# Streamed weight blocks laid out contiguously by the host: a cast load of 128 runs of 4 KB in place of 1024 runs of 512 B

## The chip, the cores and the metric

The kernel runs on all 8 cores of one Trainium2 chip, the same program on each. A core takes one prompt sequence of 2048 tokens and 16 of the 128 sampled sequences (8 tokens each, 128 rows), so 2176 rows in all; the weights are read whole by every core, each from its own copy in device memory. No data passes between cores. The metric is the device time of one execution in microseconds, that of the slowest core.

## What is computed

One layer of a convolutional decoder, cut to what matters here:

```python
u = _rmsnorm(h, g_mix)
proj = jnp.einsum('ntd,de->nte', u, w_in)       # 1024 -> 9 * 1024 columns
a_b, a_c, a_h, a_z, b_v, b_g, b_z, gate_a, gate_b = jnp.split(proj, SPLITS, axis=-1)
ya = a_b * _causal_dwconv(ext_a, w_conv_a) * silu(a_z)        # 3 taps over a_c * a_h
ya = einsum(ya, w_out_a)
c = _causal_dwconv(ext_b, w_conv_b) + b_conv_b                # 31 taps over b_v * sigmoid(b_g)
yb = silu(_layernorm(c, ln_g, ln_b)) * silu(b_z)
yb = einsum(yb, w_out_b)
h = h + einsum(sigmoid(gate_a) * ya + sigmoid(gate_b) * yb, w_o)
h = h + sigmoid(_rmsnorm(h, g_ple) @ w_pg) * (p @ w_pe)       # then a last RMSNorm
```

All inputs and outputs are float32 in device memory; the matmuls run in bfloat16, with channels on the partitions.

## The kernel before

**Blocks and stages.** The 2176 rows are taken in three blocks: 768, 768 and 640 rows (512 of the prompt and the 128 sampled ones), each in two column pieces (512 + 256, in the last block 512 + 128). A block goes through stages: s1 loads rows of `x`, takes their RMS and transposes them into `uT`; s2 makes the value and gate of branch B for a chunk of 128 channels (matmuls on L508) and applies the 31 taps as 32 small matmuls (L571), two jobs later than the projection of the same job; s3 makes the four projections of branch A (L687) and s4, two chunks after each s3 chunk from the fifth on, the gate `b_z` with the LayerNorm (L643); s5 makes both output projections and both merge gates (L779, L784, L790); s6 does `w_o`, the second RMSNorm, `w_pg`, `w_pe` (L844, L891, L897) and the store, 128 rows at a time.

**The weights that are streamed.** `w_in`, `w_out_a` and `w_out_b` don't stay on the core. They come as blocks of 1024 rows by 128 columns, cast from float32 to bfloat16 by the DMA, into a ring of 8 tiles `ring0` to `ring7` (128 partitions x 8 x 128 bfloat16). Each of the three blocks streams 88 of them: 8 groups of 2 in s2, 8 groups of 4 in s3, 8 groups of 1 in s4 and 8 groups of 4 in s5, 264 loads in the whole program. `add_group` writes the list of sources in the order of use; `wgroup` hands out the ring tiles of the next group; `wdone` marks a group as used when its last matmul is emitted and calls `pump`, which emits up to four more loads whose ring tiles are free.

**The queues.** The loads are issued by GpSimd (POOL, L288), in program order with the small copies and statistics that POOL does. A rule with four names (`swq`) makes each POOL load wait for the fourth POOL load ahead of it. SyncE (SP) issues the plain loads and stores: `x` rows (L400, L766, L824), the history `sb` and `sa`, the results, and in s2 four SBUF-to-SBUF copies per job that lay the shifted rows out for the 31 taps (`R` from `vext`, L542). `w_o`, `w_pg` and `w_pe` are loaded once, by POOL, during the first chunks of s2 in the first block (`w_o` and `w_pg` in halves of 512 rows with 4 KB of contiguous source each).

**The source of one streamed block before.** `wcol` gives a slice of 128 columns of the row-major matrix, which is 1024 pieces of 512 B that lie 36 KB apart (4 KB apart in `w_out_a` and `w_out_b`).

Of the kernel before, what the change touches and what calls it, by code (L numbers as in the profile page):

```python
# [11 lines left out]
D = 1024  # L12
NCH = 8
# [131 lines left out]
def build_program():  # L145
    nc = bass.Bass("TRN2", target_bir_lowering=False)

    def din(name, shape):
        return nc.dram_tensor(name, shape, F32, kind="ExternalInput").ap()
# [5 lines left out]
    p_d = din("p", [NTOK, 256])  # L155
    sa_d = din("sa", [32, D])
    sb_d = din("sb", [480, D])
    w_in = din("w_in", [D, 9 * D])
    w_oa = din("w_oa", [D, D])
    w_ob = din("w_ob", [D, D])  # L160
    w_o = din("w_o", [D, D])
    w_pg = din("w_pg", [D, D])
    w_pe = din("w_pe", [256, D])
# [11 lines left out]
    with contextlib.ExitStack() as st:  # L175
# [18 lines left out]
        ring = [sb(f"ring{i}", [128, NCH, 128], BF16) for i in range(NRING)]  # L194
# [65 lines left out]
        def add_group(srcs):  # L260
            WG.append(list(range(len(WL), len(WL) + len(srcs))))
            for sap in srcs:
                WL.append((sap, len(WG) - 1))

        def wcol(c0, j):
            return w_in[:, c0 * D + 128 * j:c0 * D + 128 * j + 128]

        for _bi in range(len(BLOCKS)):
            for j in range(NCH):
                add_group([wcol(4, j), wcol(5, j)])  # L270
            for j in range(NCH):
                add_group([wcol(1, j), wcol(2, j), wcol(0, j), wcol(3, j)])
                if j >= 4:
                    add_group([wcol(6, 2 * (j - 4))])
                    add_group([wcol(6, 2 * (j - 4) + 1)])
            for j in range(NCH):
                add_group([w_oa[:, 128 * j:128 * j + 128], w_ob[:, 128 * j:128 * j + 128], wcol(7, j), wcol(8, j)])
        wst = dict(nl=0, ng=0, done=set())

        def pump(maxn=4):  # L280
            nem = 0
            while nem < maxn and wst["nl"] < len(WL) and (wst["nl"] < NRING or WL[wst["nl"] - NRING][1] in wst["done"]):
                nem += 1
                t = wst["nl"]
                wst["nl"] += 1
                k = t % NRING
                src = WL[t][0]
                S.add("pool", lambda e, k=k, src=src: e.dma_start(  # L288
                    out=ring[k][:, :, :], in_=src.rearrange("(k p) m -> p k m", p=128)),
                    writes=[f"ring{k}", swq()], dma=f"ring{k}")  # L290

        def wgroup():
# [44 lines left out]
        for h in range(2):  # L337
            RESIDENT.append(lambda h=h: S.add("pool", lambda e: e.dma_start(
                out=wo_t[:, 4 * h:4 * h + 4, :],
# [687 lines left out]
```

How the kernel before makes its waits and increments, by code:

```python
            def run(engname, e):  # L101
                waited = {}
                for o in ops:
                    if o["eng"] != engname:
                        continue
                    need = {}
                    for d in o["deps"]:
                        od = ops[d]
                        v = od["seq"] * (16 if od["dma"] is not None else 1)
                        if v > need.get(od["chan"], 0):
                            need[od["chan"]] = v
                    for c, v in need.items():
                        if waited.get(c, 0) >= v:
                            continue
                        e.wait_ge(sems[c], v)
                        waited[c] = v
                    ins = o["fn"](e)
                    if o["signal"]:
                        ins.then_inc(sems[o["chan"]], 16 if o["dma"] is not None else 1)
                if engname == final_wait_eng:
                    for c, v in final.items():
                        if waited.get(c, 0) < v:
                            e.wait_ge(sems[c], v)
```

## Time and profile before

| | before |
|---|---|
| time, median of 3 runs (lowest, highest) | 1221.61 us (1203.57, 1291.15) |
| profiled execution: span of the slowest core (core 7) | 1197.9 us |
| spans of the 8 cores in it | 1191.6 to 1197.9 us |
| mean granted TensorE clock, both dies | 0.94 |
| TensorE (PE) busy | 1006.1 us, 84% |
| VectorE, ScalarE, GpSimd busy | 47%, 30%, 28% |
| DMA packets, and those under 512 B | 303514, 278993 |
| read from device memory | 172.23 MB |

The profiled execution has no time of its own beside its span; the lowest of the three runs is 5.7 us above that span. In the rows further down "a<-b" is a transfer or an instruction that writes a from b, with the numbers of ring tiles and buffers left out; the numbers after "x" count. "busy" is the time in which an engine had an instruction in work. A DMA packet's size is that of its written side: a ring load counts as 256 KB although it reads 512 KB of float32. The DMA share is the time of all packets over 16 engines; since an engine can have more than one packet in work, it can come out above 1.

### The profile page before, as it was taken

How to read it: one execution, taken by the hardware profiler on the slowest of the kernel's cores; microseconds unless marked ns; L12 is line 12 of the kernel's file. 1: busy time of each engine (PE TensorE's matmuls, PEld its weight loads, DVE VectorE, ACT ScalarE, POOL GpSimd, SP SyncE). 2: the span in 40 equal slices, each digit the busy share in tenths (PEclk: the TensorE clock that was granted, in tenths of full speed). 3: DMA queues.
4: the chain of work that ended last, by engine and by line, in shares of the span. 5: the costliest groups of instructions: out<-in, count | busy, mean ns of one | idle time of the engine just before them, and what ended most of it. 6: DMA issues, size and time to landing. Idle time of an engine off the chain costs nothing.

```text
span 1197.9 us, 20798 instructions; the slowest of 8 cores (1191.6 to 1197.9 us)
## 1 busy us (share of the span) xinstructions
PE 1006.1 (84%) x6774; PEld 563.1 (47%) x6774; DVE 565.9 (47%) x927; ACT 357.5 (30%) x661; POOL 335.5 (28%) x512
## 2 busy tenths in 40 slices
PE   1599968987999957999889799995799967789984
PEld 0355645544664424556555455542355533444542
DVE  1335426665333553454666533356465665622354
ACT  3122222233112452223222311245222223221243
POOL 4122203323332221122333233313243432323110
PEclk9999989999999977999999899998799998899998
DMA  9798689896998243677889799923498898999321
GB/s 176 122 145 110 107 167 95 81 89 60 104 106 108 79 154 49 90 90 121 81 79 95 69 106 100 114 75 126 72 128 120 78 87 84 90 132 117 36 82 75
DMA packets 303514, 119.74 MB, mean 100 GB/s; under 512 B 278993, under 2 KB 293713, under 8 KB 303377
## 3 DMA queue, kind: packets, MB, share of 16 engines
q0 software_dynamic: 279392, 75.06, 65.0%
q1 hardware_dynamic: 24017, 43.36, 11.7%
q8 instruction: 56, 0.92, 0.3%
q14 instruction: 49, 0.40, 0.1%
HBM read 172.23 MB, written 11.14 MB: 153 GB/s over the span
## 4 chain that ended last, share of the span: by engine, by line
PE 61%; DVE 11%; DMA 10%; issue 9%; ACT 6%; SPq 1%; POOL 1%; DVEq 0%; ACTq 0%; POOLq 0%
PE ps L687 13%; PE ps L571 10%; PE ps L790 9%; PE ps L508 9%; PE ps L891 6%; PE ps L779 4%; DMA t_ring<-w_in 4%; PE ps L784 4%; PE ps L844 3%; DMA t_R_1<-t_vext 3%; DMA t_xs<-x 2%; DVE t_tmp L721 2%; DVE t_tmp L653 1%; DVE t_cbuf L663 1%; ACT t_tmp L661 1%
## 5 line engine op out<-in xcount | busy, mean ns | idle before, releaser
L288 POOL DMA_DIRECT2D t_ring<-w_in x216 | 191.0, 890 | 434.3 <-PE ps L508 196.2
L687 PE MATMUL ps<-t_uT,t_ring 128*128 128x512 bf16 (+2 forms) x1536 | 253.1, 327 | 46.5 <-DMA t_ring<-w_in 17.3
L687 PEld LDWEIGHTS ps<-t_uT,t_ring 128*128 128x128 bf16 x1536 | 142.1, 100 | 156.6 <-issue 65.7
L571 PE MATMUL ps<-t_R_0,t_Wp 128*64 128x512 bf16 (+2 forms) x768 | 135.9, 331 | 9.3 <-DMA t_R_0<-t_vext 9.3
L571 PE MATMUL ps<-t_R_1,t_Wp 128*64 128x512 bf16 (+2 forms) x768 | 134.6, 331 | 7.3 <-DMA t_R_1<-t_vext 7.3
L508 PE MATMUL ps<-t_uT,t_ring 128*128 128x512 bf16 (+2 forms) x768 | 129.5, 324 | 0.3 <-DVE t_uT L426 0.3
L790 PE MATMUL ps<-t_uT,t_ring 128*128 128x512 bf16 (+2 forms) x768 | 129.5, 323 | 0.0
L571 PEld LDWEIGHTS ps<-t_R_0,t_Wp 128*64 128x64 bf16 x768 | 77.0, 113 | 53.8 <-issue 21.7
L891 PE MATMUL ps<-t_wpg_t,t_u2T 128*128 128x512 bf16 x272 | 74.3, 436 | 29.8 <-DVE t_u2T L867 20.8
L508 PEld LDWEIGHTS ps<-t_uT,t_ring 128*128 128x128 bf16 x768 | 68.2, 99 | 58.5 <-issue 17.3
L790 PEld LDWEIGHTS ps<-t_uT,t_ring 128*128 128x128 bf16 x768 | 71.0, 99 | 50.9 <-issue 5.2
L801 DVE TENSOR_TENSOR t_tmp<-ps,t_tmp 128x512 f32<-128x512 f32 (+2 forms) x48 | 25.7, 534 | 130.0 <-ACT t_tmp L797 130.0
L571 PEld LDWEIGHTS ps<-t_R_1,t_Wp 128*64 128x64 bf16 x768 | 77.1, 113 | 16.7 <-issue 15.8
L779 PE MATMUL ps<-t_yaT,t_ring 128*128 128x512 bf16 (+2 forms) x384 | 69.8, 326 | 12.8 <-DMA t_ring<-w_in 5.4
L784 PE MATMUL ps<-t_cbuf,t_ring 128*128 128x512 bf16 (+2 forms) x384 | 68.3, 320 | 8.8 <-DVE t_cbuf L663 8.8
L657 ACT ACTIVATE t_tmp<-t_tmp,t_vecs 128x512 f32<-128x512 f32 (+2 forms) x48 | 33.0, 688 | 125.3 <-DVE t_tmp L653 125.3
L797 ACT ACTIVATE t_tmp<-ps 128x512 f32<-128x512 f32 (+2 forms) x48 | 22.7, 473 | 149.9 <-PE ps L790 149.1
L312 POOL TENSOR_SCALAR t_msq<-t_ssq 128x1 f32<-128x1 f32 x51 | 10.7, 210 | 196.8 <-ACT t_xs L309 138.6
L422 PE MATMUL ps<-t_idb,t_xb 128*128 128x128 bf16 x136 | 15.6, 285 | 59.3 <-ACT t_xb L417 59.3
L578 ACT ACTIVATE t_cbuf<-ps,t_vecs 128x512 f32<-128x512 f32 (+2 forms) x48 | 27.0, 563 | 123.5 <-PE ps L571 123.5
L891 PEld LDWEIGHTS ps<-t_wpg_t,t_u2T 128*128 128x128 bf16 x272 | 28.8, 109 | 72.9 <-issue 51.9
L844 PE MATMUL ps<-t_wo_t,t_cbuf 128*128 128x512 bf16 x272 | 61.0, 379 | 0.0
(121 smaller groups left out, 1291.5 us busy)
## 6 DMA issues: line engine op xcount, KB each, us to landing
t_ring<-w_in POOLq DMA_DIRECT2D x216, 256.0 KB, 7.2
t_xs<-x SPq DMA_DIRECT2D x34, 512.0 KB, 4.1
y<-t_yt SPq DMA_DIRECT2D x17, 512.0 KB, 2.7
t_ring<-w_oa POOLq DMA_DIRECT2D x24, 256.0 KB, 6.5
t_ring<-w_ob POOLq DMA_DIRECT2D x24, 256.0 KB, 7.0
t_R_0<-t_vext SPq DMA_DIRECT2D x48, 67.8 KB, 2.0
t_R_1<-t_vext SPq DMA_DIRECT2D x48, 67.8 KB, 2.0
t_wo_t<-w_o POOLq DMA_DIRECT2D x2, 1024.0 KB, 11.0
```

The lines of the kernel that those rows point to most:

```text
L288: S.add("pool", lambda e, k=k, src=src: e.dma_start(out=ring[k][:, :, :], in_=src.rearrange("(k p) m -> p k m", p=128)), writes=[f"ring{k} ...
L508: S.add("pe", lambda e, b=b, kw=kw, k=k, off=off, n=n: e.matmul(ps[:, b, 0:n], lhsT=ring[kw][:, k, :], rhs=uT[:, k, off:off + n], start=(k ...
L571: S.add("pe", lambda e, bc=bc, ds=ds, i=i, g=g, rhs=rhs, n=n: e.matmul(ps[64 * g:64 * g + 64, bc, 0:n], lhsT=Wp[ds][:, 16 * g + i, :], rhs ...
L578: S.add("act", lambda e, bc=bc, j=j, off=off, n=n: e.activation(out=cbuf[:, j, off:off + n], in_=ps[:, bc, 0:n], func=AF.Identity, bias=vc ...
L657: S.add("act", lambda e, tx=tx, tl=tl, j=j, n=n: e.activation(out=tmp[tl][:, 0:n], in_=tmp[tx][:, 0:n], func=AF.Silu, scale=vcol(V_LNG, j) ...
L687: S.add("pe", lambda e, b=b, kw=kw, k=k, off=off, n=n: e.matmul(ps[:, b, 0:n], lhsT=ring[kw][:, k, :], rhs=uT[:, k, off:off + n], start=(k ...
L779: S.add("pe", lambda e, pya=pya, ka=ka, k=k, off=off, n=n: e.matmul(ps[:, pya, 0:n], lhsT=ring[ka][:, k, :], rhs=yaT[:, k, off:off + n], s ...
L784: S.add("pe", lambda e, pyb=pyb, kbb=kbb, k=k, off=off, n=n: e.matmul(ps[:, pyb, 0:n], lhsT=ring[kbb][:, k, :], rhs=cbufb[:, k, 2 * off:2 ...
L790: S.add("pe", lambda e, b=b, kw=kw, k=k, off=off, n=n: e.matmul(ps[:, b, 0:n], lhsT=ring[kw][:, k, :], rhs=uT[:, k, off:off + n], start=(k ...
L801: S.add("dve", lambda e, pya=pya, ta=ta, n=n: e.tensor_tensor(out=tmp[ta][:, 0:n], in0=ps[:, pya, 0:n], in1=tmp[ta][:, 0:n], op=ALU.mult), ...
L844: S.add("pe", lambda e, h=h, k=k, bm=bm, mcol=mcol: e.matmul(ps[:, bm[h], :], lhsT=cbufb[:, k, mcol:mcol + 128], rhs=wo_t[:, k, 512 * h:51 ...
L891: S.add("pe", lambda e, h=h, k=k, bg=bg: e.matmul(ps[:, bg[h], :], lhsT=u2T[:, k, :], rhs=wpg_t[:, k, 512 * h:512 * h + 512], start=(k == ...
```

## The change

The host now hands `w_in`, `w_out_a` and `w_out_b` over as one array of blocks: block n holds the 128 columns n*128 to n*128+127, and in it row p (of 128) holds, one after another, the 8 pieces of 128 values that go to partition p of the ring tile. So a load reads 128 rows of 4 KB that follow on each other (512 KB without a gap) and writes 128 rows of 2 KB. The bytes, the number of loads, the ring, its order, the waits and every instruction on every engine stay as they are: set side by side, the lists of TensorE, VectorE and ScalarE are the same, and that of GpSimd has the same 373 rows in the same order, with `128x1024` in place of `128x8x128` as the shape of the ring loads. `w_o`, `w_pg` and `w_pe` are not touched. The re-layout is done by the host before the launch.

```diff
-    w_in = din("w_in", [D, 9 * D])
-    w_oa = din("w_oa", [D, D])
-    w_ob = din("w_ob", [D, D])
+    w_in = din("w_in", [9 * NCH, 128, D])
+    w_oa = din("w_oa", [NCH, 128, D])
+    w_ob = din("w_ob", [NCH, 128, D])
...
         def wcol(c0, j):
-            return w_in[:, c0 * D + 128 * j:c0 * D + 128 * j + 128]
+            return w_in[c0 * NCH + j, :, :]
...
-                add_group([w_oa[:, 128 * j:128 * j + 128], w_ob[:, 128 * j:128 * j + 128], wcol(7, j), wcol(8, j)])
+                add_group([w_oa[j, :, :], w_ob[j, :, :], wcol(7, j), wcol(8, j)])
...
                 S.add("pool", lambda e, k=k, src=src: e.dma_start(
-                    out=ring[k][:, :, :], in_=src.rearrange("(k p) m -> p k m", p=128)),
+                    out=ring[k][:, :, :].rearrange("p k m -> p (k m)"), in_=src),
                     writes=[f"ring{k}", swq()], dma=f"ring{k}")
...
+    def tiled(w):
+        w = f(w)
+        n = w.shape[1] // 128
+        return np.ascontiguousarray(w.reshape(8, 128, n, 128).transpose(2, 1, 0, 3)).reshape(n, 128, D)
+
+    shared = dict(w_in=tiled(w_in[0]), w_oa=tiled(w_out_a[0]), w_ob=tiled(w_out_b[0]), w_o=f(w_o[0]), w_pg=f(w_pg[0]),
```

## Rows read from the trace of the kernel before

**Rows 1.** The page's part 3, DMA queues: packets, MB written, share of 16 engines
```profile
q0 software_dynamic: 279392, 75.06, 65.0%
```

**Rows 2.** The page's part 4, the chain that ended last, by engine
```profile
PE 61%; DVE 11%; DMA 10%; issue 9%; ACT 6%; SPq 1%; POOL 1%; DVEq 0%; ACTq 0%; POOLq 0%
```

**Rows 3.** Waits of core 7: engine, line, waited for; us in total, times, longest
```profile
PE ps L687 <- DMA t_ring<-w_in: 17.3, 6, 6.6
...
PE ps L571 <- DMA t_R_0<-t_vext: 9.3, 4, 3.7
...
PE ps L571 <- DMA t_R_1<-t_vext: 7.3, 5, 3.1
...
PE ps L779 <- DMA t_ring<-w_in: 5.4, 4, 2.1
```

**Rows 4.** The same view for core 4
```profile
PE ps L571 <- DMA t_R_0<-t_vext: 10.5, 5, 3.7
PE ps L571 <- DMA t_R_1<-t_vext: 10.1, 5, 4.4
...
PE ps L360 <- DMA t_Abuf<-sb: 8.3, 1, 8.3
PE ps L687 <- DMA t_ring<-w_in: 8.0, 3, 5.0
```

**Rows 5.** Core 7's chain in order of time: start us, us, what
```profile
15.61 9.37 DMA t_xs<-x
...
27.36 8.13 DMA t_xs<-x
...
49.00 7.79 DMA t_R_1<-t_vext
...
852.13 5.92 DMA t_R_1<-t_vext
...
979.89 10.14 DMA t_ring<-w_in
...
1062.60 9.24 DMA t_ring<-w_in
```

**Rows 6.** Core 7 by stretch: length, busy us per engine, PEclk, DMA share, GB/s
```profile
301.00:304.00 3.00, 3.00 (x15) 1.37 (x14) 0.69 (x1) 0.60 (x1) 0.00 (x0) 1.00 1.81 179
...
42.00:46.00 4.00, 4.00 (x18) 1.83 (x17) 1.80 (x1) 0.36 (x1) 0.00 (x0) 1.00 1.09 199
981.00:987.00 6.00, 3.08 (x27) 1.75 (x24) 4.40 (x10) 0.90 (x2) 1.74 (x3) 1.00 1.06 88
```

**Rows 7.** The page's part 6, DMA issues: count, KB written, us from issue to landing
```profile
t_ring<-w_in POOLq DMA_DIRECT2D x216, 256.0 KB, 7.2
t_xs<-x SPq DMA_DIRECT2D x34, 512.0 KB, 4.1
...
t_R_0<-t_vext SPq DMA_DIRECT2D x48, 67.8 KB, 2.0
...
t_wo_t<-w_o POOLq DMA_DIRECT2D x2, 1024.0 KB, 11.0
```

**Rows 8.** POOL's groups by shape: count, busy us, mean ns of one
```profile
L288 POOL DMA_DIRECT2D t_ring<-w_in x216 | 191.0, 890 | 434.3 <-PE ps L508 196.2 <-PE ps L687 160.6 <-DMA t_ring<-w_in 30.1
...
L830 POOL DMA_DIRECT2D t_pbt<-p x11 | 6.7, 609 | 0.5
```

**Rows 9.** By stretch as in Rows 6: matmuls after the wait that ended at 990.6
```profile
990.60:996.00 5.40, 5.36 (x13) 1.90 (x14) 2.17 (x5) 1.95 (x4) 1.17 (x3) 0.50 1.12 108
996.00:1002.00 6.00, 6.00 (x52) 3.62 (x51) 1.48 (x3) 1.47 (x3) 0.78 (x2) 0.99 0.00 0
```

**Rows 10.** By stretch: s3 with s4, first block
```profile
206.00:285.00 79.00, 68.43 (x399) 39.43 (x399) 53.02 (x100) 22.35 (x44) 25.07 (x35) 0.98 0.94 88
```

**Rows 11.** DMA issues between 64 and 96 us: count, KB each, median us to landing
```profile
t_R_1<-t_vext SPq DMA_DIRECT2D x6, 35.8 KB, 7.9
```

**Rows 12.** Core 7's chain: two successive chunks of s2 in the second block
```profile
489.40 3.56 PE ps L508 x16
...
500.25 3.56 PE ps L508 x16
```

More of the change, by code:

```diff
@@ L997 @@
     ident = np.eye(128, dtype=np.float32)
-    shared = dict(w_in=f(w_in[0]), w_oa=f(w_out_a[0]), w_ob=f(w_out_b[0]), w_o=f(w_o[0]), w_pg=f(w_pg[0]),
+    def tiled(w):
[3 more added lines that the diff above has]
+    shared = dict(w_in=tiled(w_in[0]), w_oa=tiled(w_out_a[0]), w_ob=tiled(w_out_b[0]), w_o=f(w_o[0]), w_pg=f(w_pg[0]),
                   w_pe=f(w_pe[0]), vecs=vecs, gfin=gfin, ident=ident)
```

## The prediction

> **What bounds the kernel now.** I read the DMA queues first. GpSimd's queue takes 65% of 16 engines' time [rows 1], nearly all of it in ring loads (264 x 1024 = 270336 of its 279392 packets), which looks as if the DMA engines were the bound. The chain that ended last says otherwise: 61% TensorE, 11% VectorE, 10% DMA [rows 2]. So transfers hold the end back for about 120 of 1197.9 us, and only that part can move. Third, the waits of TensorE itself: on core 7 it stood 17.3 + 5.4 = 22.7 us for ring tiles and 9.3 + 7.3 = 16.6 us for the shifted rows `R` [rows 3]; on core 4, whose span is 0.7 us shorter, 8.0 us for ring tiles on L687, 20.6 us for `R` and 8.3 us for `sb` [rows 4]. The reader should see that the cores reach nearly the same end by different waits. Fourth, the chain in order of time shows where the transfers sit: two `x` loads at the start, of 9.37 and 8.13 us; `R` copies of 7.79 us at 49 us and 5.92 us at the start of the third block; ring loads of 10.14 and 9.24 us in the third block [rows 5]. An `x` load takes 4.1 us in the median and an `R` copy 2.0 us [rows 7], so the long ones wait behind something, and in each of those places ring loads are in flight.
>
> Last, the speed of a ring load, by stretch. Between 301 and 304 us ring loads run alone at 179 GB/s written with a DMA share of 1.81. Between 42 and 46 us half of `w_o` runs, with the very rows that the change gives the ring loads (4 KB read, 2 KB written): 199 GB/s at a share of 1.09 [rows 6]. So the share of 65% overstates the occupation: the small packets overlap, and at its best the old form is only 11% slower. But the old form isn't always at its best: between 981 and 987 us, with ring loads waiting and hardly anything else on this core's queues, it moves 88 GB/s [rows 6], half as much. What slows it there is outside this core's queues; that other cores' reads do it is a guess.
>
> **The change part by part.** The order, the waits and the bytes stay. What changes is the packets (264 x 896 = 236544 fewer), the issue and the speed.
>
> Issue: a ring load holds POOL for 890 ns, a `p` load with 128 rows 609 ns [rows 8]. I take 0.6 us, so 264 x 0.29 = 77 us less POOL time. POOL is busy 28% of the span and waits for TensorE most of the rest, so this is worth nothing except ahead of an exposed group of four, 4 x 0.29 = 1.2 us, counted below. If POOL's cover were gone, the whole 77 us would count.
>
> Transfer of one ring load (262144 B written): 1.46 us at 179 GB/s, 3.0 us at 88 GB/s; the new form 1.32 us at 199 GB/s. What the new form does where the old one drops to 88 no row shows. Below: it drops as much, 2.7 us; above: it doesn't drop, 1.32 us. I take 1.5, near the `w_o` row, since that row was read while the other cores loaded their `w_o` too.
>
> By the Trainium skill's page "DMA: Bandwidth & Descriptors", section "Why small descriptors are slow (HBM only)", each packet carries about 3 cycles over size/32; eight packets of 256 B then need 88 cycles and one of 2 KB 67, a factor of 1.31, where the trace has 1.11 between its two undisturbed streams. By the page one load would come to 1.1 us (an estimate), and the sum below would gain at most 2 us more.
>
> A group of four from its first issue to its last landing: now three issues of 0.89 us and the 9.24 us of the last load [rows 5, 8], 11.9 us, while TensorE needs 8.7 us for one s5 group of the third block (32 matmuls of 512 and of 128 columns). New: the first load like an `x` load (the same 128 rows of 4 KB, 4.1 us) plus 0.3 us for the longer issue, then three at 1.4: 8.6 us. Bounds: 8.4 us, and the 11.0 us of `w_o`, which is four such loads in one [rows 7]. I take 8.6, 3.3 us less per exposed group.
>
> Sum for core 7. *Ring waits*: ten, of 22.7 us; the two long ones (6.6 and 4.1 us) shrink by 3.3 each and the other eight, 12.0 us, nearly go: 18 us. After a long wait TensorE runs at a granted clock of 0.50, its lower level, for 5.4 us, then 0.99 [rows 9]; that costs 2.7 us each time. With shorter waits I count 3 us back in all. *Start*: both `x` loads share the engines with the first eight ring loads; alone they would take 4.1 us, so the bounds are 0 and 9.3 us; I take 7, since eight loads at 1.4 us are nearly through when the second `x` load is issued. *R*: the copies stand behind one pair of ring loads (and, four times, behind a piece of `w_o` or `w_pg`, which stays); bounds 0 and 16.6 us; I take half, 8. *sb*: four ring loads ahead of it become shorter; 2 us. Together 38 us.
>
> Core 4 by the same steps: ring 8, clock 1, start 6, `R` 10 of 20.6, `sb` 3 of 8.3: 28 us. The time is that of the slowest core, so the gain is nearer to core 4's: 32 us less the little that cores drift apart. Against span plus surroundings, 1197.9 + 5.7 = 1203.6 us (the lowest run; the median shown is 18 us above it, and I predict for executions like the profiled one), the sum is 1203.6 - 32 = 1171.6, so **1171 us**. Late next is VectorE: in s3 with s4 of the first block TensorE is busy 68.4 of 79 us without a ring wait, the chain running through VectorE and ScalarE [rows 10].
>
> **The rivals.**
>
> *All waits on transfers go.* Ring waits with their clock (22.7 + 5.4), the start (9.3), `R` (16.6) and `sb` (2.4) on core 7 are 56 us; the same on core 4 is about 46. Time 1203.6 - 50 = 1153. For it: 88 GB/s could be the old form's weakness alone. Against it: `w_pg` still stands ahead of `R`, where copies took 7.9 us [rows 11], and after the first projection of a block no work covers the copy.
>
> *The waits pass to VectorE.* If the s3 and s4 ring waits only uncover the chain of rows 10, what remains is s5's 5.4, start 4, `R` 4, `sb` 1: 14 us, time 1189. For it: in the first block the same stage loses 10.6 us of 79 with no ring wait.
>
> *Bytes bound the loads.* The load of a core runs as fast as the memory gives it and the stall at 88 GB/s stays; only the earlier issue counts, 1.2 us for each of six exposed groups: 7 us, time 1196. For it: the undisturbed streams differ by 11%. Against it: 199 GB/s written was reached. The page named above gives, in "Where 436 GB/s comes from", about 358 GB/s per core from HBM as what binds. Ring loads at 179 GB/s written read just 358 GB/s; but `w_o` read 398 GB/s, so the trace bears the rule out only in part.
>
> *Slower: `R` copies starve.* A row of 2 KB holds an engine longer than one of 256 B. In s2 a copy has cover: a chunk takes 500.25 - 489.40 = 10.85 us [rows 12], the copies are issued some 3.2 us into it, so landing within 7.6 us is hidden. Behind `w_pg`, the same rows, they took 7.9 us [rows 11]. If a pair of ring loads did that, and 2 us more, in each of the 24 chunks, 48 us would be lost against 14 won: 1238. It decides from a landing of 7.6 us on. Against it: `w_pg` is as many bytes as four ring loads, a pair half of that, and ahead of `R` there now stand the same bytes in smaller rows.
>
> **How the numbers follow.** Chances: the sum as worked out 0.55 (own range 1160 to 1184), all waits go 0.15, passed to VectorE 0.18, bytes 0.08, starved copies 0.04. The predicted time is that of the first. The range leaves out the lower half of the second case (0.07), most of the fourth (0.06) and the fifth: 1140 to 1197. About 2% is what a measurement of this kernel tells from no change; against 1203.6 that is 1179.5. Four fifths of the first case and the whole second lie below it: 0.60 faster. The third, fourth and the rest of the first make 0.36 the same; slower 0.04.
>
> **What would show it.** Right: GpSimd's queue at 42848 packets and a share near 35% with unchanged MB; ring issues near 0.6 us, landing median near 5 us in place of 7.2; TensorE's waits for ring tiles under 6 us on every core; the two `x` pieces at the start under 6 us; no stretch of ring loads below 150 GB/s. Wrong towards bytes: stretches at 88 GB/s remain. Wrong towards VectorE: ring waits gone, but s3 with s4 of the third block as long as before. Wrong towards starving: `R` landings above 7.6 us outside the first 100 us. The step I trust least is the 1.5 us of a load where the old form drops to 88 GB/s; next is the half that I took for `R`.

## The result, and the profile after

The changed kernel takes 1179.67 us (median of 4 runs, 1177.29 to 1208.40) where the kernel before, on the same chip and in the same series, takes 1219.42 us (median of 4, 1203.57 to 1291.15). The ratio is 0.971 with a 95% interval of 0.964 to 0.978: about 3% faster. On another chip the same kernel came out at 0.978 (experiment e0), so 2 to 3% is what the change is worth. Ratios leave out executions in which the cores of one die run at a lower granted clock, so a median can stand beside a far higher maximum.

| profiled execution | before | after |
|---|---|---|
| span of the slowest core | 1197.9 us (core 7) | 1178.2 us (core 4) |
| span of core 7 | 1197.9 us | 1174.3 us |
| span of core 4 | 1197.2 us | 1178.2 us |
| mean clock of core 7, of core 4 | 0.944, 0.941 | 0.941, 0.949 |
| DMA packets of GpSimd's queue | 279392 | 42848 |

The page of the kernel after, of its slowest core (core 4). The first line is GpSimd's DMA queue (packets, MB written, share of 16 engines), the second the chain that ended last by engine, the last three are DMA issues (count, KB written, median us to landing):

```profile
q0 software_dynamic: 42848, 75.06, 42.1%
...
PE 64%; DVE 11%; issue 9%; ACT 7%; DMA 7%; SPq 1%; DVEq 0%; POOL 0%; ACTq 0%; POOLq 0%
...
t_ring<-w_in POOLq DMA_DIRECT2D x216, 256.0 KB, 5.6
t_xs<-x SPq DMA_DIRECT2D x34, 512.0 KB, 4.2
...
t_wo_t<-w_o POOLq DMA_DIRECT2D x2, 1024.0 KB, 10.3
```

Beside [rows 1, 2, 7]: the packets are those foretold, the bytes are unchanged, a ring load lands in 5.6 us in place of 7.2, and the chain goes through DMA for 7% of the span in place of 10%. An `x` load, whose form didn't change, takes what it took (4.2 us against 4.1), and a half of `w_o` hardly less (10.3 against 11.0).

TensorE's waits for transfers on core 7 (engine, line, waited for; us in total, times, longest), to be read against [rows 3]:

```profile
PE ps L571 <- DMA t_R_1<-t_vext: 8.3, 3, 4.7
PE ps L571 <- DMA t_R_0<-t_vext: 7.3, 3, 3.4
...
PE ps L360 <- DMA t_Abuf<-sb: 3.5, 1, 3.5
...
PE ps L687 <- DMA t_ring<-w_in: 2.0, 1, 2.0
...
PE ps L779 <- DMA t_ring<-w_in: 0.3, 1, 0.3
```

And on core 4, against [rows 4], with one line of the kernel before that [rows 4] doesn't have:

```profile
PE ps L687 <- ACT t_tmp L661: 17.3, 7, 3.5
```

After:

```profile
PE ps L687 <- ACT t_tmp L661: 22.1, 9, 3.0
...
PE ps L571 <- DMA t_R_0<-t_vext: 8.7, 4, 3.6
PE ps L571 <- DMA t_R_1<-t_vext: 7.5, 3, 4.3
...
PE ps L687 <- DMA t_ring<-w_in: 5.2, 4, 1.9
...
PE ps L360 <- DMA t_Abuf<-sb: 4.7, 1, 4.7
```

The waits for ring tiles fell on core 7 from 22.7 to 2.3 us; the waits for `R` hardly moved (16.6 to 15.6 on core 7, 20.6 to 16.2 on core 4). The largest wait of L687 is now, on every core, the one for ScalarE's `t_tmp`: on core 7 it took the place of the ring tiles, on core 4 it was the largest before and grew from 17.3 to 22.1 us.

Where the 19.7 us of span came from. The table is worked out from the two traces: a stage lasts from its first matmul to the first matmul of the next one (a, b, c are the three blocks; s1a counts from the start of the span; s3 is cut at its fifth chunk, where s4 joins in), and each number is the median over the 8 cores.

| us | s1a | s2a | s3a, first half | s2b | s2c | s3c with s4 | s5c | s6c | all others |
|---|---|---|---|---|---|---|---|---|---|
| before | 37.8 | 99.1 | 69.5 | 88.8 | 76.0 | 74.1 | 79.0 | 69.0 | 600.8 |
| after | 35.1 | 95.6 | 67.3 | 87.0 | 74.9 | 70.3 | 74.0 | 70.1 | 599.9 |

The third block's s3 with s4 and its s5, where the ring waits were, gave 8.8 us, the start 2.7, the three s2 stages 6.4, the first half of s3a, where `sb` is waited for, 2.2; s6c, which has no ring load, is 1.1 longer.

What TensorE did with that time, also worked out from the two traces (two cores lack the same 95 matmuls in both, so the busy times are a little low on both sides):

| mean of the 8 cores | before | after |
|---|---|---|
| span, us | 1195.1 | 1173.4 |
| TensorE busy, us | 1006.4 | 998.8 |
| its waits for ring tiles | 13.0 | 3.5 |
| for `R` | 18.9 | 15.3 |
| for `sb` and `sa` | 8.9 | 6.0 |
| for ScalarE (without `xb` of s1) | 34.0 | 38.7 |
| for VectorE | 45.4 | 42.6 |

So 9.5 us came out of the ring waits, and nearly as much, 7.6, out of the matmuls themselves: TensorE needed less time for the same work, since a higher clock was granted to it, on seven of the eight cores. Before:

```profile
die 0 (median of its cores): 1195.3 us, clock 0.941
die 1 (median of its cores): 1194.9 us, clock 0.942
```

and after:

```profile
die 0 (median of its cores): 1173.6 us, clock 0.949
die 1 (median of its cores): 1174.5 us, clock 0.948
```

Half of the 7.6 us lies in s3c with s4. There the ring waits fell from 7.2 to 3.2 us on the mean of the cores and the waits for ScalarE rose from 7.7 to 11.7, so that TensorE stood idle as long as before; what got shorter is its busy time, 59.5 to 55.7 us, at a granted clock of 0.97 in place of 0.91. In s5c the ring waits went from 3.7 to 0.2 and little took their place (the stage is 5.2 us shorter, 0.8 of it busy time).

### The profile page after: what moved, and what is told of

It reads as the page before. It is cut to its first block, busy times and chain, and to the rows that moved or that the text cites. A ratio compares the mean times of both kernels' runs of the same rounds, so it can differ in the third digit from the quotient of the medians.

```text
span 1178.2 us, 20798 instructions; the slowest of 8 cores (1166.8 to 1178.2 us)
## 1 busy us (share of the span) xinstructions
PE 1000.9 (85%) x6774; PEld 562.7 (48%) x6774; DVE 560.9 (48%) x927; ACT 356.5 (30%) x661; POOL 231.0 (20%) x512
## 3 DMA queue, kind: packets, MB, share of 16 engines
q0 software_dynamic: 42848, 75.06, 42.1%
q1 hardware_dynamic: 24017, 43.36, 12.2%
## 4 chain that ended last, share of the span: by engine, by line
PE 64%; DVE 11%; issue 9%; ACT 7%; DMA 7%; SPq 1%; DVEq 0%; POOL 0%; ACTq 0%; POOLq 0%
PE ps L687 13%; PE ps L571 10%; PE ps L790 10%; PE ps L508 9%; PE ps L891 6%; PE ps L779 5%; PE ps L784 5%; PE ps L643 3%; PE ps L844 3%; DMA t_xs<-x 2%; DMA t_R_1<-t_vext 2%; ACT t_tmp L661 2%; DVE t_cbuf L663 2%; DVE t_tmp L653 2%; DVE t_tmp L650 1%
## 5 line engine op out<-in xcount | busy, mean ns | idle before, releaser
L687 PE MATMUL ps<-t_uT,t_ring 128*128 128x512 bf16 (+2 forms) x1536 | 254.6, 328 | 40.8 <-ACT t_tmp L661 22.1
L687 PEld LDWEIGHTS ps<-t_uT,t_ring 128*128 128x128 bf16 x1536 | 143.9, 101 | 150.1 <-issue 53.1
L288 POOL DMA_DIRECT2D t_ring<-w_in x216 | 115.7, 536 | 479.4 <-PE ps L508 213.8
L571 PE MATMUL ps<-t_R_0,t_Wp 128*64 128x512 bf16 (+2 forms) x768 | 132.5, 326 | 8.7 <-DMA t_R_0<-t_vext 8.7
L571 PE MATMUL ps<-t_R_1,t_Wp 128*64 128x512 bf16 (+2 forms) x768 | 131.7, 326 | 7.5 <-DMA t_R_1<-t_vext 7.5
L508 PE MATMUL ps<-t_uT,t_ring 128*128 128x512 bf16 (+2 forms) x768 | 130.3, 325 | 0.3 <-DVE t_uT L426 0.3
L790 PE MATMUL ps<-t_uT,t_ring 128*128 128x512 bf16 (+2 forms) x768 | 128.9, 322 | 0.0
L571 PEld LDWEIGHTS ps<-t_R_0,t_Wp 128*64 128x64 bf16 x768 | 75.8, 111 | 53.2 <-issue 21.1
L571 PEld LDWEIGHTS ps<-t_R_1,t_Wp 128*64 128x64 bf16 x768 | 75.9, 111 | 15.1 <-issue 13.3
L797 ACT ACTIVATE t_tmp<-ps 128x512 f32<-128x512 f32 (+2 forms) x48 | 22.7, 473 | 143.1 <-PE ps L790 142.3
L891 PEld LDWEIGHTS ps<-t_wpg_t,t_u2T 128*128 128x128 bf16 x272 | 28.5, 108 | 74.1 <-issue 52.5
L422 PE MATMUL ps<-t_idb,t_xb 128*128 128x128 bf16 x136 | 15.6, 285 | 56.0 <-ACT t_xb L417 56.0
L643 PE MATMUL ps<-t_uT,t_ring 128*128 128x512 bf16 (+2 forms) x384 | 60.9, 317 | 0.0
## 6 DMA issues: line engine op xcount, KB each, us to landing
t_wo_t<-w_o POOLq DMA_DIRECT2D x2, 1024.0 KB, 10.3
```

Of the source, the lines that this page charges most:

```text
L288: S.add("pool", lambda e, k=k, src=src: e.dma_start(out=ring[k][:, :, :].rearrange("p k m -> p (k m)"), in_=src), writes=[f"ring{k}", swq( ...
L508: S.add("pe", lambda e, b=b, kw=kw, k=k, off=off, n=n: e.matmul(ps[:, b, 0:n], lhsT=ring[kw][:, k, :], rhs=uT[:, k, off:off + n], start=(k ...
L571: S.add("pe", lambda e, bc=bc, ds=ds, i=i, g=g, rhs=rhs, n=n: e.matmul(ps[64 * g:64 * g + 64, bc, 0:n], lhsT=Wp[ds][:, 16 * g + i, :], rhs ...
L643: S.add("pe", lambda e, pz=pz, kz=kz, k=k, off=off, n=n: e.matmul(ps[:, pz, 0:n], lhsT=ring[kz][:, k, :], rhs=uT[:, k, off:off + n], start ...
L687: S.add("pe", lambda e, b=b, kw=kw, k=k, off=off, n=n: e.matmul(ps[:, b, 0:n], lhsT=ring[kw][:, k, :], rhs=uT[:, k, off:off + n], start=(k ...
L790: S.add("pe", lambda e, b=b, kw=kw, k=k, off=off, n=n: e.matmul(ps[:, b, 0:n], lhsT=ring[kw][:, k, :], rhs=uT[:, k, off:off + n], start=(k ...
```

## The experiments

All were compared with the kernel before in runs on the same chip; e0 to e3 share one chip, e4 to e7 a second, e8 to e11 a third. The median of before there was 1210.94, 1211.05 and 1212.47 us, so kernels of different chips are set side by side by their ratio.

### e0: the changed kernel on another chip

> The changed kernel once more, so that the next three have it beside them on one chip. Every theory: 0.971 of the kernel before (0.965 to 0.978), about 1179 us; TensorE's waits for ring tiles 2 to 6 us on each core, its waits for R copies still 12 to 17 us, ring issues 0.53 us each on POOL.

Measured: 1183.29 us, ratio 0.978 (0.973 to 0.983). The two intervals overlap, and the kernels below are set against both ratios, 0.971 and 0.978.

### e1 and e2: packets or distance

The change does two things to a block's source: it makes one packet of eight, and it brings the pieces together. e1 does the second alone, 1024 runs of 512 B that fill 512 KB without a gap:

```diff
-    w_in = din("w_in", [9 * NCH, 128, D])
+    w_in = din("w_in", [9 * NCH, D, 128])
...
-                    out=ring[k][:, :, :].rearrange("p k m -> p (k m)"), in_=src),
+                    out=ring[k][:, :, :], in_=src.rearrange("(k p) m -> p k m", p=128)),
...
```

(`w_oa`, `w_ob` and the host's re-layout follow suit, here and in e2 and e11.)

> The host lays a block out as one piece of 512 KB, but with the packets of the kernel before: 1024 runs of 512 B. Three theories of what made the ring loads slow. Apart (the 512 B pieces lie 36 KB apart in memory): as fast as the changed kernel, ratio 0.97 to 0.98, ring loads never below 150 GB/s for some us. Packets (8 times as many small packets): no gain, 0.99 to 1.0, stretches of 85 to 110 GB/s remain and the landing median stays near 7 us. Issue (0.88 us against 0.53 us of POOL's time for one load): no gain either, 0.99 to 1.0, but with streams near 179 GB/s throughout. In every theory POOL's issue is back at 0.88 us.

e2 does the first alone, 128 runs of 4 KB that lie 288 KB apart:

```diff
-    w_in = din("w_in", [9 * NCH, 128, D])
...
+    w_in = din("w_in", [128, 9 * NCH, D])
...
-            return w_in[c0 * NCH + j, :, :]
+            return w_in[:, c0 * NCH + j, :]
...
```

> The other half: 128 runs of 4 KB, as in the changed kernel, but with the 128 runs of a load 288 KB apart (32 KB in the two output projections). Apart: most of the gain is lost, 0.985 to 1.0. Packets and issue: as the changed kernel, 0.97 to 0.98, issue 0.53 us and landing median 5.6 us.

Measured: e1 1202.05 us, ratio 0.993 (0.990 to 0.996); e2 1184.63 us, ratio 0.979 (0.975 to 0.984). The queue and the landing of a ring load on the page of e1:

```profile
q0 software_dynamic: 279392, 75.06, 64.3%
...
t_ring<-w_in POOLq DMA_DIRECT2D x216, 256.0 KB, 6.3
```

and on that of e2:

```profile
q0 software_dynamic: 42848, 75.06, 42.0%
...
t_ring<-w_in POOLq DMA_DIRECT2D x216, 256.0 KB, 5.4
```

The long runs give the gain wherever they lie; bringing short runs together gives 0.7%. The fewer packets did it, not the neighbourhood.

### e3: is it the cheaper issue?

```diff
+        junk = sb("junk", [128, 240], BF16)
...
+                S.add("pool", lambda e: e.memset(junk[:], 0.0), writes=["junk"])
                 S.add("pool", lambda e, k=k, src=src: e.dma_start(
```

> The changed kernel with a POOL memset of about 0.34 us ahead of each ring load, so that a load costs POOL what it cost before (0.88 us). Issue: the gain goes, 0.99 to 1.0. Apart and packets: at most 4 us slower than the changed kernel, 0.97 to 0.976, since POOL waits for TensorE most of the time.

Measured: ratio 0.980 (0.973 to 0.987). GpSimd's groups (count, busy us, mean ns of one):

```profile
L290 POOL DMA_DIRECT2D t_ring<-w_in x216 | 115.0, 532 | 428.1 <-PE ps L510 203.7 <-PE ps L689 161.1 <-PE ps L645 16.7
L289 POOL MEMSET t_junk<- 128x240 bf16 x264 | 84.2, 319 | 0.0
```

With the fill a load costs POOL 532 + 319 = 851 ns, close to the 890 of before, and the gain is still there. The 0.35 us a load that the change takes off POOL (94 us in all on core 4) are worth nothing that can be measured; the ratio of the changed kernel on this chip is 0.978.

### e11: half way

A block as two halves, 256 runs of 2 KB:

```diff
-    w_in = din("w_in", [9 * NCH, 128, D])
...
+    w_in = din("w_in", [9 * NCH, 256, 512])
...
-                    out=ring[k][:, :, :].rearrange("p k m -> p (k m)"), in_=src),
+                    out=ring[k][:, :, :].rearrange("p (h k) m -> p h (k m)", h=2),
+                    in_=src.rearrange("(h p) m -> p h m", p=128)),
...
```

> Each streamed block lies as two halves of 128 runs of 2 KB (256 runs a load; 1 KB written a run) instead of 128 runs of 4 KB. Theory 'the run costs, whatever its length': the fixed part falls by three quarters where the change takes seven eighths, so nearly all of the gain is there: ratio 0.976 to 0.981, q0 near 42% to 47%, landing near 5.6 us. Rival 'only the longest packets do': a ratio half way to the load of 1024 runs in one place (0.993), 0.984 to 0.988, landing near 6 us.

Measured: 1186.04 us, ratio 0.982 (0.977 to 0.987). Queue, issue and landing on its page:

```profile
q0 software_dynamic: 76640, 75.06, 46.0%
...
L288 POOL DMA_DIRECT2D t_ring<-w_in x216 | 154.1, 716 | 449.3 <-PE ps L509 204.3
...
t_ring<-w_in POOLq DMA_DIRECT2D x216, 256.0 KB, 5.6
```

Share and landing are those of the first theory, the ratio falls between the two ranges. Of the way from e1 (0.993) to the long runs (0.978) it has three quarters, and of the packets it takes away six sevenths; within the intervals that is the same. So it doesn't separate the theories by time.

### e4: what is left in the ring loads

From the ninth load on only an eighth of each block is brought (the matmuls then use stale weights):

```diff
-                S.add("pool", lambda e, k=k, src=src: e.dma_start(
-                    out=ring[k][:, :, :].rearrange("p k m -> p (k m)"), in_=src),
+                nk = NCH if t < NRING else 1
+                S.add("pool", lambda e, k=k, src=src, nk=nk: e.dma_start(
+                    out=ring[k][:, 0:nk, :].rearrange("p k m -> p (k m)"), in_=src[:, 0:128 * nk]),
```

> The changed kernel, but every ring load after the first 8 brings only the first 512 B of each row, an eighth of the bytes (the later matmuls then use old weights, so the results are not the layer's). It asks what all ring transfers together still cost. Theory that transfers still hold the end back (R copies and x rows behind ring loads, the last ring waits): 20 to 28 us less than the changed kernel, ratio to the kernel before about 0.955 to 0.96, waits of TensorE for R under 8 us. Theory that what is left is VectorE's chain and the waits without a ring load in front: at most 8 us less, 0.97 or more.

Measured: 1168.48 us (1166.08 to 1169.57), ratio 0.964 (0.960 to 0.969), between the two expectations. Core 4's waits for transfers, all of them:

```profile
PE ps L572 <- DMA t_R<-t_vext: 6.8, 5, 5.1
PE ps L361 <- DMA t_Abuf<-sb: 3.3, 1, 3.3
PE ps L375 <- DMA t_Abuf<-sa: 1.2, 1, 1.2
```

No ring tile is waited for, on any core, and yet only about 12 us are gained on the changed kernel (1180.63 us on this chip, see e5; by the ratios 8 to 17). By stage the gain is 3.4, 3.9 and 4.0 us in the three s2 and 0.8 in s5c; s3c with s4 takes 70.1 us against 70.3. TensorE's waits for `R` fall from 15.3 to 8.2 us on the mean of the cores. So after the change the ring loads cost their remainder almost wholly by standing ahead of the `R` copies. The third block's s3 with s4 is at its floor: without any ring wait TensorE waits 12.7 us for ScalarE there.

### e5: an experiment that missed

```diff
-                    wdone(wg_)
+                    if j == 0:
+                        wst["done"].add(wg_)
+                    else:
+                        wdone(wg_)
```

> The changed kernel, but the two ring loads that the first chunk of each block sets free are issued with those of the second chunk, so that the first R copies of a block have no ring load in front. Theory that R copies wait behind ring loads whatever their rows: the pieces of some 5.2 us at the start of the second and third block become 2 to 3 us, 2 to 3 us less for each block, 5 to 8 us less in all than the changed kernel. Rival, that the copies are late by themselves (their issue on SP, the first use): no change within 2 us and landings still near 5 us.

Measured: 1180.63 us, ratio 0.974 (0.970 to 0.978), every stage within 0.7 us of the changed kernel. It says nothing on its question: the two loads moved behind other work in the order of emission, but POOL had nothing to do in between, and issued them (core 4) at 455.82 and 456.69 us, beside the first `R` copies as before; the copy on the chain still took 5.18 us at 456.96 us. To hold a load back it needs a wait (e8). So e5 is in effect the changed kernel on the second chip.

### e6: the start

The first eight ring loads go out as four at the start and two after each of the first `x` tiles. Here two go out at the start and the other six from the fourth `x` tile on:

```diff
-        pump()
+        pump(2)
...
-            pump(2)
+            if tl[0][0] > 0 or ti >= 3:
+                pump(2)
```

> The changed kernel, but at the start only two ring loads are issued at once and the other six after the fourth tile of x rows. Theory that the x rows of the start stand behind ring loads: the pieces of 7.5 and 5.7 us in the chain become 4.1 to 4.5 us, and s2 begins 4 to 5 us earlier. Rival, that the other cores' reads of x or the serial work on ScalarE set the pace: at most 1 us.

Measured: 1177.97 us, ratio 0.975 (0.968 to 0.982). The `x` loads issued between 14 and 24 us in e6, core 4 (count, KB, median us to landing):

```profile
t_xs<-x SPq DMA_DIRECT2D x3, 512.0 KB, 3.5
```

and in the kernel after between 14 and 30 us, with the four ring loads that went out beside them:

```profile
t_xs<-x SPq DMA_DIRECT2D x3, 512.0 KB, 7.5
t_ring<-w_in POOLq DMA_DIRECT2D x4, 256.0 KB, 8.8
```

s1a goes from 35.1 to 30.9 us with s2a as before (95.9). Over the 8 cores these three `x` loads took 9.5, 9.1 and 6.7 us in the kernel before, 7.5, 8.1 and 5.5 after, and 3.5 to 3.6 in e6: of what they lost beside ring loads, the longer rows took off less than a third, and the order takes off all. That the whole kernel gains by it is not separated from its interval.

### e7: `w_o` and `w_pg` in pieces

Sixteen loads of 128 rows, one with each job of s2 from the fourth on (two from the fifteenth), in place of four loads of 512 rows in the first chunks:

```diff
-                out=wo_t[:, 4 * h:4 * h + 4, :],
-                in_=w_o[512 * h:512 * h + 512, :].rearrange("(k p) m -> p k m", p=128)),
+                out=wo_t[:, q, :], in_=w_o[128 * q:128 * q + 128, :]),
...
+                if bi == 0 and 3 <= idx:
+                    for _ in range(1 if idx < 14 else 2):
+                        if RESIDENT:
+                            RESIDENT.pop(0)()
```

> The changed kernel, but w_o and w_pg are loaded in 16 pieces of 128 rows, one for each job of s2 in the first block from the fourth job on, in place of four pieces of 512 rows in its first four chunks. Theory that R copies of the first block wait behind these pieces: waits of TensorE for R 5 to 8 us less in the first 100 us, 3 to 6 us less time. Rival: the pieces only move the wait into later chunks, no change within 2 us.

Measured: 1177.27 us, ratio 0.974 (0.969 to 0.979). Core 4's waits:

```profile
PE ps L358 <- DMA t_Abuf<-sb: 8.2, 1, 8.2
PE ps L567 <- DMA t_R<-t_vext: 8.2, 6, 3.0
```

s2a is 6.4 us shorter (89.2) and the waits for `R` are halved (16.2 to 8.2), but the last pieces now stand ahead of `sb`, whose wait goes from 4.7 to 8.2 us, and the first half of s3a is 4.1 us longer (71.4). The gain of one stage is the next one's wait.

### e8: a ring pair that waits for `R`

The loads that the first chunk of a block frees wait until the first job's four `R` copies have landed:

```diff
-        def pump(maxn=4):
+        def pump(maxn=4, also=()):
...
-                    writes=[f"ring{k}", swq()], dma=f"ring{k}")
+                    reads=also, writes=[f"ring{k}", swq()], dma=f"ring{k}")
...
-                    wdone(wg_)
+                    wdone(wg_, [f"R0_{g}_{jj}" for g in range(2) for jj in range(2)] if j == 0 else ())
```

> The changed kernel, with one wait more: the two pairs of ring loads that the first chunk of each block of s2 frees are issued only once the first job's four R copies have landed. Bytes, packets and all other work are those of the changed kernel. Theory 'R copies queue behind the ring loads': in the changed kernel two copies of the first job land in 5.3 and 5.2 us at 459 and 845 us on core 4, beside a ring pair issued at the same time; alone they land in about 2 us. Then those two pieces fall to 2 to 3 us, PE's waits on R_0 and R_1 fall by 4 to 8 us on a core, s2b and s2c are each 2 to 3 us shorter, and the kernel is 4 to 8 us faster than the changed one: ratio to before 0.966 to 0.972. Rival 'the first job waits for something else, or the ring loads pay for it later': the pieces fall but ring waits rise by as much, no stage changes by over 1 us, ratio 0.973 to 0.979.

Measured: 1176.62 us, ratio 0.975 (0.969 to 0.980); s2a 94.1, s2b 85.0, s2c 71.8 us, that is 1.5, 2.0 and 3.1 us less than the changed kernel. Two pieces of core 4's chain in the second block (start us, us, what):

```profile
452.77 1.99 DMA t_R<-t_vext
457.31 4.33 DMA t_R<-t_vext
```

The changed kernel has one piece of 5.34 us there, at 459.31. The first copy now takes what it takes alone, so it did queue behind the ring pair; the pair, 0.6 us later, then holds up the second job's copies. It is the same on every core: the slowest copy of the first job in the second and third block landed after 5.4 us in the kernel before, 5.1 after, 2.3 in e4 and 2.0 in e8 (medians). The mechanism is shown by piece and stage (6.6 us over three stages; on the mean of the cores TensorE's waits for `R` fall by 4.5 us and those for ring tiles stay where they were, 3.5 and 3.6); the total doesn't stand out from its interval.

### e9 and e10: the order of the loads, with the new layout and without

e9 is the changed kernel with the edits of e6 and e8 and, in place of e7's order of the pieces, ten of them with the jobs of s2 and the rest with the chunks of s5 in the first block (the second of the two places below). e10 is the same order with the old 1024-run loads.

```diff
+                if bi == 0 and 3 <= idx <= 12 and RESIDENT:
+                    RESIDENT.pop(0)()
...
+                if bi == 0 and RESIDENT:
+                    RESIDENT.pop(0)()
```

> The changed kernel with three edits to the order of its loads together: R copies ahead of the ring pair (as in e8), two ring loads instead of eight at the start so that x tiles come first (as in e6), and w_o and w_pg in sixteen loads of 128 rows, one with each of ten jobs of s2 in block 0 and the rest with the chunks of s5 (e7 had them bunched ahead of s3). The same bytes. If the three places are independent: s1a 4 us shorter, s2a 6 us shorter with s3a no longer than in the changed kernel (67 us), s2b and s2c 2 to 3 us shorter each: 12 to 16 us in all, 1164 to 1168 us, ratio 0.960 to 0.965. If what is gained in one stage is waited for in the next (as in e6 and e7): 0.971 to 0.976.

> The kernel before (1024 runs of 512 B) with the same three edits to the order of its loads as e9, and without the new layout. It tells how much of the layout's gain is one that order alone would have given. Theory 'two separate gains': before loses 9 us in s3c and s5c, where the ring loads come too slowly while they flow, and order does not mend that; s1a and s2a get shorter by 5 to 10 us together: 1190 to 1197 us on this chip's scale, ratio 0.983 to 0.99, and e9 is still 2% below it. Rival 'the layout only cleared the collisions that order clears as well': ratio 0.965 to 0.975, within 1% of e9.

Measured: e9 1166.07 us (median of 7, 1162.34 to 1209.78), ratio 0.965 (0.960 to 0.970), the fastest kernel here with all of its work and what its first theory expected. e10 1191.51 us, ratio 0.980 (0.974 to 0.986), between its two expectations: s1a and s2a give 14.7 us where 5 to 10 were expected, and e9 is 1.5% below it. By stage, medians over the cores:

| us | s1a | s2a | s3a, first half | s2b | s2c | s3c with s4 | s5c |
|---|---|---|---|---|---|---|---|
| before | 37.8 | 99.1 | 69.5 | 88.8 | 76.0 | 74.1 | 79.0 |
| after | 35.1 | 95.6 | 67.3 | 87.0 | 74.9 | 70.3 | 74.0 |
| e10: order alone | 30.5 | 91.7 | 68.8 | 86.8 | 74.0 | 73.9 | 81.2 |
| e9: order and layout | 30.9 | 86.3 | 66.9 | 84.7 | 71.6 | 71.7 | 74.5 |

Core 6 of e10, its slowest, still waits for ring tiles:

```profile
PE ps L568 <- DMA t_R<-t_vext: 10.5, 10, 3.6
PE ps L780 <- DMA t_ring<-w_in: 7.3, 3, 3.2
...
PE ps L684 <- DMA t_ring<-w_in: 4.5, 5, 1.9
```

and core 7 of e9, its slowest, hardly does (on the mean of the cores the ring waits are 17.2 us in e10 and 4.8 in e9, against 13.0 before and 3.5 after):

```profile
PE ps L568 <- DMA t_R<-t_vext: 5.4, 5, 2.2
...
PE ps L684 <- DMA t_ring<-w_in: 0.9, 1, 0.9
```

The order alone is worth 2.0%, the layout alone 2.2 to 2.9%, both together 3.5%. So they overlap, by about a quarter at the middle of intervals of half a per cent: both clear the start, where the order without the layout gets all (30.5 us). They are separate in s5c, where the order gains nothing (81.2 us against 79.0) and the layout 5.0 (on its own) or 6.7 (on top of the order). e9's gains by stage on the changed kernel add up to 19 us in s1a and the three s2; 13.7 arrive in the span, since s3c with s4 gives 1.4 back and s6c 0.7, and the rest is spread over stages and cores.

## Why the prediction was right, and by which steps

The time came out at 1179.67 us where 1171 was forecast: within the range of the main case (1160 to 1184), and on the side of "faster". Term by term, on the two cores of the sum (us less; the start is the length of s1a, the clock TensorE's busy time):

| | core 7: forecast | measured | core 4: forecast | measured |
|---|---|---|---|---|
| ring waits | 18 | 20.4 | 8 | 3.6 |
| clock | 3 | -0.4 | 1 | 8.4 |
| start | 7 | 5.5 | 6 | 1.9 |
| `R` | 8 | 1.0 | 10 | 4.4 |
| `sb` | 2 | 2.4 | 3 | 3.6 |
| sum | 38 | 28.9 | 28 | 21.9 |
| span | | 23.6 | | 19.0 |

What lies between the sum and the span are waits for other engines, which moved both ways (those for ScalarE grew by 6.4 us on core 7 and 2.8 on core 4); the sum has no term for them.

The mechanism held, and several sizes did not. In ratios the forecast looks better than it was: 1171.6 / 1203.6 is 0.973, measured 0.971 and 0.978, while between the two profiled executions 19.7 us were gained where the sum had 32. The base makes up for it. The 5.7 us of "surroundings" were the difference between two executions: wherever a time and the spans of its cores are both on record, the time is 1.5 to 1.7 us above the slowest core. The profiled execution of before thus took about 1199.5 us, less than any of the 35 executions of before with a time here (1202.76 us and up). Against the usual execution the gain is 28 to 35 us (means 1211.4 to 1182.9 us on e0's chip, 1214.1 to 1178.9 in the first series). So two errors partly cancel, and that is luck. That the rows of before had less of the loss in them than a usual execution has is the likely reading; no second trace of it was taken.

**What bounds: right.** A queue at 65% that took 42% afterwards gave 20 us, not a third of the time. The chain's 10% through DMA was the right measure, as an upper bound; it is 7% now.

**Speed of a load: right, but not everywhere.** Ring loads of the kernel after, core 4, in a stretch where they run alone (the stretch, its length, busy us of PE, PEld, DVE, ACT and POOL, PEclk, DMA share, GB/s):

```profile
1027.00:1030.00 3.00, 2.22 (x21) 1.54 (x18) 2.58 (x7) 0.00 (x0) 0.62 (x2) 1.00 1.13 203
```

and in a slow one, on core 5:

```profile
1013.00:1016.00 3.00, 2.88 (x14) 1.09 (x12) 1.59 (x3) 1.11 (x3) 0.00 (x0) 1.00 0.45 54
```

At 203 GB/s a load takes 1.29 us; the undisturbed gain over [rows 6] is 203 / 179 = 1.13. The prediction's factor of 1.31 by the Trainium skill's cycles a packet ("DMA: Bandwidth & Descriptors", "Why small descriptors are slow (HBM only)") is not reached here. It was worked out with the sizes written, 256 B and 2 KB; with the sizes read, 512 B and 4 KB, the same cycles give 152 against 131, a factor of 1.16 (an estimate), which this trace is near; no run here tells which size counts. The Trainium skill's 358 GB/s a core ("DMA: Bandwidth & Descriptors", "Where 436 GB/s comes from") isn't a limit in this trace: 203 GB/s written from float32 are 406 read. A group of four took 8.8 us from its first issue (960.33 us) to its last landing (969.15) on core 4; 8.6 was forecast, and 8.7 is the median of such groups on all cores (10.3 before). But "no stretch below 150 GB/s" was wrong. Of all windows of 3 us (stepped by 1 us, 8 cores) in which throughout some ring load had been under way for 2 us and no other transfer was, 17% lay below 110 GB/s before and 6% after, 57% and 25% below 150. The slow stretches became rarer and did not go; that other cores' reads cause them was not tried.

**Ring waits: right on core 7, not on core 4.** On core 7 20.4 of 22.7 us went, on core 4 3.6 of 9.2, where nearly all were counted: there the loads still wait behind each other at the end of s3c. Two pieces of core 4's chain, the second behind an `x` load as well:

```profile
990.32 5.14 DMA t_ring<-w_in
...
1045.92 8.48 DMA t_ring<-w_in
```

**The clock: right in direction, and too small.** 3 us were forecast on core 7, which got nothing, and 1 on core 4, which got 8.4; the mean of the eight cores is 7.6. By stretch, s3c with s4 and s6c of core 7, before:

```profile
970.90:1049.70 78.80, 59.45 (x392) 31.54 (x392) 46.52 (x101) 20.33 (x44) 26.45 (x45) 0.90 0.96 91
...
1130.40:1197.90 67.50, 46.45 (x258) 22.77 (x255) 32.22 (x39) 27.05 (x48) 9.23 (x23) 0.95 0.22 70
```

and after:

```profile
959.80:1030.30 70.50, 56.51 (x393) 30.95 (x394) 45.38 (x100) 20.22 (x44) 18.21 (x44) 0.95 0.64 102
...
1103.70:1174.30 70.60, 50.16 (x256) 23.65 (x254) 32.15 (x39) 27.19 (x48) 9.20 (x23) 0.87 0.21 67
```

Where core 7's ring waits went the granted clock rose from 0.90 to 0.95, and TensorE needed 2.9 us less for the same matmuls (and 2.3 less in s5c). In s6c, which the change doesn't touch, it needed 3.7 us more, at 0.87 in place of 0.95. That is no price of the change: on the mean of the cores the granted clock of s6c is 0.90 before and 0.89 after, and core 7's 0.95 was the highest of the eight before. Why the clock of s6c differs from core to core (0.86 to 0.95 before, 0.87 to 0.94 after) is not shown. The gain isn't one execution's either: in the executions that the ratios use, the mean granted clock of the cores is 0.940 to 0.941 for the kernel before on the three chips of e0 to e11, and 0.947 and 0.946 for the changed kernel in its two.

**Start: mis-sized.** 7 and 6 us were forecast, 5.5 and 1.9 came. Core 4's chain after:

```profile
14.96 7.49 DMA t_xs<-x
...
24.84 5.66 DMA t_xs<-x
```

"Under 6 us" holds for one of the two. The reason given, that eight loads of 1.4 us are nearly through when the second `x` load is issued, fails twice over: the first four ring loads landed only between 13.96 and 19.86 us, beside three `x` loads, and the other four of the eight were issued from 14.84 us on, beside the `x` loads on the chain; e6 moves those and gets the 4.2 us that the layout didn't. Some `x` loads even got slower by the change: the second and third of the start, issued at 2.9 and 3.4 us, land after 9.5 and 12.3 us in place of 8.1 and 9.8 (medians over the cores). They are not on the chain.

**`R`: mis-sized.** Half of 16.6 and 20.6 us was taken; 1.0 and 4.4 went (3.6 on the mean of the cores). The copy after the first projection of a block still lands behind the ring pair:

```profile
459.31 5.34 DMA t_R_0<-t_vext
...
845.43 5.18 DMA t_R_0<-t_vext
```

and between 64 and 96 us on core 7, behind `w_pg`, a copy takes 6.4 us where [rows 11] has 7.9:

```profile
t_R_1<-t_vext SPq DMA_DIRECT2D x4, 35.8 KB, 6.4
```

An undisturbed pair of ring loads is only 13% faster than before, so what queues behind it is hardly helped; the forecast probably carried the gain of the disturbed loads over to a place where they weren't disturbed. e4, e7 and e8 show that the waits go when bytes or order change. The starved-copies rival stayed away too: outside the first 100 us the longest landing of an `R` copy, on any core, fell from 7.9 to 6.8 us.

**`sb`: right** in size: 2 and 3 forecast, 2.4 and 3.6 gone.

**Issue: right in what it is worth** (nothing, e3). GpSimd's groups on core 4 after:

```profile
L288 POOL DMA_DIRECT2D t_ring<-w_in x216 | 115.7, 536 | 479.4 <-PE ps L508 213.8 <-PE ps L687 166.9 <-issue 29.7
```

0.54 us, a little under the 0.6 guessed from the `p` load.

**Share and landing:** 42.1% against "near 35%" and 5.6 us against 5, the former because a core's flow still slows down, and a packet then counts for longer: at the undisturbed 1.13 for 203 GB/s the 75.06 MB would make 35%, while the slow stretch has 0.45 for 54.

**The rivals.** *All waits go* (1153): no; with an eighth of the bytes it is still 1168 (e4). *Passed to VectorE* (1189): right about the waits, wrong about the time. In s3c with s4 the 4.0 us that ring waits lost came back whole as waits for ScalarE, in the chain that the rival named; on all of L687 the ring waits fell from 9.2 to 3.3 us and those for `t_tmp` (L661) grew from 15.7 to 22.4 (means of the cores). The stage still got 3.8 us shorter, to 0.2 us above e4's, which has no ring wait; by its account that is TensorE's busy time at the higher clock. Whether the clock or the shorter ring waits alone would have brought the stage to that floor is not separated: e4 stands there at a granted clock of 0.93, three cores of the kernel after at 1.00. *Bytes bound* (1196): e1 and e2 have the same bytes and differ by 1.4%, so no, although slow stretches remain.

## What to carry to other kernels

A DMA queue's share tells neither what it costs nor what fewer packets will bring: read the waits that it ends, ask of each whether it waits for the speed of the loads or for its place behind them, and count on the layout for the first kind only. Of the first kind, ask too what the engine will wait for next, and count the clock that comes back when the long waits go. For the second kind the order of the issues is the remedy, with the bytes left as they are (e9 on top of the layout: from about 0.975 to 0.965). And look at where the profiled execution lies among the runs before making a sum against it: here it was the fastest.

## What the runs showed of the hardware that was not expected

- Runs of 512 B that follow on each other are hardly better than runs 36 KB apart (0.993, landing 6.3 us), and runs of 4 KB that lie 288 KB apart as good as joined ones (0.979 and 0.978, landing 5.4 and 5.6 us).
- The issue of a load on GpSimd is not in proportion to its runs: 536 ns for 128, 716 for 256, 890 for 1024.
- A copy from one place of the core's memory to another, 2.0 us alone, takes some 5 us beside two ring loads of 256 KB, whether those come as 2048 packets (5.4) or as 256 (5.1), and 2.3 beside two loads of an eighth of the bytes.
- The ring loads of one core can fall to 54 GB/s for 3 us with nothing else in flight on it, with packets of 2 KB as well. What slows them stays open.
- Loads of longer rows can hold up a neighbour more: the second and third `x` load of the start, issued just before the first ring loads, took 9.5 and 12.3 us beside 4 KB rows and 8.1 and 9.8 beside 512 B pieces (e6, with 4 KB rows: 9.6 and 12.2; e10, with 512 B pieces: 8.2 and 9.8). Why was not tried.
- Shorter waits paid twice: TensorE's mean granted clock rose from 0.941 to 0.948 (mean of the cores), and it needed 7.6 us less for the same matmuls, against 9.5 us less of ring waits. In s3c with s4 its idle time did not change, only who it waited for.
